# A decoder trunk on one Trainium2 core: each attention item's values product is issued four steps of the projection later, together with the next item's scores, and its output is taken two steps behind it

## The reference

```python
z = rms_norm(x, g_mix) @ w_in + b_in
q, k, v, u, vg = jnp.split(z, SPLITS, axis=-1)
scores = jnp.einsum('bnqhgd,bnshd->bnhgqs', qb, kb) * ATTN_SCALE      # 128-blocks, this one and the one before
probs = sink_softmax(scores, mask, sinks)
out = jnp.einsum('bnhgqs,bnshd->bnqhgd', probs, vb)
vg = layer_norm(gelu(vg), ...); gm_out = gelu(u) * chunk_spatial_mix(vg, gm_w_s, gm_b_s)
x = x + jnp.concatenate([attn_out, gm_out], axis=-1) @ w_out + b_out
```

## Time and profile before

| | |
|---|---|
| median of 3 runs | 986.0 us (lowest 985.79, highest 986.68) |
| profiled execution: its time / its span | 986.51 us / 984.8 us |
| TensorE busy | 963.6 us (98%) |
| VectorE, ScalarE, GpSimd busy | 672.4, 458.7, 260.5 us |
| the part that the change touches | about 416 to 515 us of the span |

### The profile page before, as it was taken

How to read it: one execution, slowest core, us unless ns; L and a number is a source line. 1 busy time by engine, 2 the same in 40 slices (tenths; PEclk the granted TensorE clock), 3 DMA queues, 4 the chain that set the end, 5 groups by cost and what they waited for, 6 DMA issues and landing times.

```text
span 984.8 us, 19296 instructions
## 1 busy us (share of the span) xinstructions
PE 963.6 (98%) x7949; PEld 947.1 (96%) x7949; DVE 672.4 (68%) x1063; ACT 458.7 (47%) x750; POOL 260.5 (26%) x150
## 2 busy tenths in 40 slices
PE   6999999999999999999999999999999999999997
PEld 4999999999999999999899999999999999999997
DVE  5899658856768654457775399857766758855576
ACT  6645425533435443566444455424543443545243
POOL 2302202211111226332318411301221211114521
PEclk9999999999999999999999999999999999999999
DMA  7962433252243336321114693253324325235202
GB/s 216 163 127 70 124 105 99 76 145 72 75 128 99 97 85 184 102 65 44 44 55 129 128 172 97 61 145 97 96 80 116 97 60 144 65 98 161 87 22 88
DMA packets 191603, 101.38 MB, mean 103 GB/s; under 512 B 12955, under 2 KB 189429, under 8 KB 191501
## 3 DMA queue, kind: packets, MB, share of 16 engines
q1 hardware_dynamic: 175904, 90.23, 32.2%
q0 software_dynamic: 11440, 5.77, 4.7%
q10 hardware_dynamic: 4172, 4.15, 1.4%
HBM read 97.59 MB, written 3.59 MB: 103 GB/s over the span
## 4 chain that ended last, share of the span: by engine, by line
PE 91%; DVE 5%; ACT 1%; DMA 1%; issue 1%; SPq 0%; DVEq 0%; ACTq 0%
PE ps L1723 49%; PE ps L1803 36%; PE ps L2141 2%; PE ps L1759 1%; DMA x_rows<-in_x_prompt_dram 1%; PE ps L2015 1%; PE ps L2044 1%; DVE w_lo L1327 0%; PE ps L1754 0%; DVE w_lo L1419 0%; PE ps L1748 0%; DVE xb_lo L1216 0%; DVE tt L1437 0%; DVE mix_lo L1550 0%; PE ps L2165 0%
## 5 line engine op out<-in xcount | busy, mean ns | idle before, releaser
L1803 PE MATMUL ps<-xo_hi,w_hi 128*128 128x260 f32 x1008 | 284.2, 282 | 0.7 <-DVE ab L1350 0.7
L1803 PE MATMUL ps<-xo_lo,w_hi 128*128 128x260 f32 x1008 | 284.7, 282 | 0.0
L1803 PE MATMUL ps<-xo_hi,w_lo 128*128 128x260 f32 x1008 | 284.4, 282 | 0.0
L1723 PE MATMUL ps<-h_hi,w_hi 128*128 128x260 f32 x960 | 195.8, 285 | 0.7 <-issue 0.6
L1723 PE MATMUL ps<-h_hi,w_lo 128*128 128x260 f32 x960 | 193.4, 283 | 0.0
L1723 PE MATMUL ps<-h_lo,w_hi 128*128 128x260 f32 x960 | 193.4, 283 | 0.0
L1803 PEld LDWEIGHTS ps<-xo_hi,w_hi 128*128 128x128 f32 x1008 | 189.6, 188 | 0.9 <-issue 0.9
L1803 PEld LDWEIGHTS ps<-xo_hi,w_lo 128*128 128x128 f32 x1008 | 189.8, 188 | 0.0
L1803 PEld LDWEIGHTS ps<-xo_lo,w_hi 128*128 128x128 f32 x1008 | 189.7, 188 | 0.0
L1723 PEld LDWEIGHTS ps<-h_hi,w_hi 128*128 128x128 f32 x960 | 148.1, 189 | 1.7 <-issue 1.2
L1723 PEld LDWEIGHTS ps<-h_lo,w_hi 128*128 128x128 f32 x960 | 148.8, 189 | 0.0
(11 more groups left out here) (276 smaller groups left out, 1476.5 us busy)
## 6 DMA issues: line engine op xcount, KB each, us to landing
w_raw<-in_w_ffn_dram SPq DMA_DIRECT2D x88, 256.0 KB, 3.0
w_a<-in_w_ffn_dram SPq DMA_DIRECT2D x36, 512.0 KB, 4.8
w_raw<-in_w_ffn_dram SPq DMA_DIRECT2D x48, 384.0 KB, 3.2
w_raw<-in_w_ffn_dram SPq DMA_DIRECT2D x16, 512.0 KB, 7.0
w_lo<-in_w_ffn_dram POOLq DMA_DIRECT2D x11, 512.0 KB, 8.4
w_raw<-in_w_in_dram SPq DMA_DIRECT2D x10, 512.0 KB, 4.0
w_raw<-in_w_ple_gate_dram SPq DMA_DIRECT2D x8, 512.0 KB, 3.6
x_rows<-in_x_prompt_dram SPq DMA_DIRECT2D x4, 512.0 KB, 5.7
```

Source lines behind the costliest of these rows:

```text
L1723: ins = pe.matmul(ps[:, bank + step * h, 0:HALF], w[:, c, w0:w0 + P], m_[:, sk, h * HALF:(h + 1) * HALF], start=(first and n == 0), stop=( ...
L1803: ins = pe.matmul(ps[:, b, 0:Q], w[:, c, k * P:(k + 1) * P], m_[:, op, k, :], start=(first and k == 0 and n == 0), stop=(k == 3 and n == 2 ...
```

## The change

The two last steps of each item are put elsewhere in the list: `values` from (u+1, 7) to (u+2, 3), `o_take` from (u+2, 2) to (u+2, 5). They are put in a loop of their own behind the first, and `put` inserts in front, so `values` of item i stands ahead of `scores` of item i+2 and `p_turn` of item i+1, and `o_take` ahead of `p_turn` r = 1 of item i+1. Behind line 320 every line number of the changed kernel is one higher.

```diff
         put(u + 1, 5, ("p_turn", i, 1))
-        put(u + 1, 7, ("values", i))
-        put(u + 2, 2, ("o_take", i))
+    for i, u in enumerate(ITEM_UNIT):
+        put(u + 2, 3, ("values", i))
+        put(u + 2, 5, ("o_take", i))
```

## The result

The changed kernel took 987.86 us (median of 22 runs, 986.2 to 989.05), the kernel before 986.07 on the same chip (22 runs, 985.09 to 988.01). The ratio is 1.0016, with a 95% interval of 1.0010 to 1.0023: 1.6 us slower (1.0 to 2.3). The forecast was 989.8, 3.8 slower, with a range of 987.0 to 992.3. So the sign was right and the time lies in the range, but the cost is less than half of what the sum gave, and it is inside the 0.2% for which I gave only 0.13.

What follows compares the result with a forecast made beforehand. TensorE was taken to bound up to 470 us, then mostly VectorE's mixer chain. Hand-over delays net of joins ended at +2.1, the half clock added 1.7: +3.8 on the median 986.0 gives 989.8 us, range 987.0 to 992.3.

Steps and rivals of the forecast that it cites:

- Joins: TensorE, items 0 to 5: values joined to scores in one insertion save 0.2 us each, -1.2 in all.
- The hand-over in units 7 and 9: o_take's copy behind L711 delays VectorE's remainder, soft and gelu_end; TensorE waits 1.5 us for g_t, twice.
- `ws_sum`, g3, `s_new`: Units 8 to 12: ws_sum waits 0.7 us, g3's turning comes 1.9 later, s_new 2.9 later, TensorE waits 1.8 for it.
- The last stretch: VectorE's part up to the release at 514.87: takes over the 2.9 us lag, less corrections, ending +2.1.
- The clock: TensorE at half clock behind its last wait, for mix_lo, where the chain is on TensorE: +1.7 us (0 to 1.9).
- The wait for `mix_lo`: TensorE, mixer's last stretch: grows from 1.0 to about 3 us, and half clock follows it.
- Rival (b): Hold-up as counted, but no half clock behind the last wait, or hidden as before: 988.1 us; chance 0.27.
- The sign that I had named: If the forecast waits are there and the time is under 988 us, the clock term is wrong.

Runs made afterwards that it cites:

- e6: Kernel of e2 with values at k-step 2 instead of 3, in an insertion of their own; 983.58 us, ratio 0.9971 to the kernel before.
- e2: Changed kernel with o_take split: ScalarE's copy stays at k-step 5, VectorE's remainder at k-step 7 behind the softmax; 982.13 us, again 982.05.
- e3: Changed kernel with values left in their old place (u+1, 7), only o_take moved to (u+2, 5); 988.37 us.
- e5: Kernel of e1 with the weights' split (w_hi, w_lo) at k-step 6 instead of 4 in all units; 992.92 us.
- e1: Changed kernel with o_take one k-step earlier, (u+2, 4) instead of (u+2, 5), so ScalarE's copy precedes the weights' copy; 987.71 us.
- e9: Kernel before, with only VectorE's remainder of the output moved to k-step 7 behind the softmax; values and ScalarE's copy left; 987.45 us.
- e7: Kernel before, with only the weights' split moved to k-step 6 instead of 4 in units 9 and 11; 988.35 us.
- e8: Kernel of e2 with the weights' split at k-step 6 instead of 4 in all units; 989.18 us.
- e4: Changed kernel with items 1, 3 and 5 left as before, only items 0, 2, 4, 6 and 7 changed; 986.39 us, ratio 0.9999.
- e10: Changed kernel once more, unaltered, one profiled execution to see where TensorE's clock falls; 986.92 us.

## Why the prediction was right or wrong

**Joins: right.** Item 1's values and item 3's scores, with the turning behind them, took 2.46 us of TensorE as one insertion (431.90 to 434.84, less two pairs of the projection at 0.24). Before, they took 1.22 (428.71 to 430.41) and 1.44 (432.79 to 434.71) apart, each less two pairs. That is 0.2 per join, as forecast. The time of e6 is in keeping with six of them.

**The hand-over in units 7 and 9: right in mechanism, in place and nearly in size.** Forecast two waits of 1.5 for `g_t`, measured two of 1.3. The profile counts the idle time from the end of the last pair of the projection; from start to start TensorE lost 1.44 us in unit 7 (the pair at 438.39, its 0.24, and 440.07), against 1.55. The difference is the link from L711 to what stands behind it: I took 1.09 us from the earlier trace rows, and it was 0.95 (435.60 to 436.55). I had misread that row: by TensorE's row the turning before it ended at 436.53 (435.93 + 0.60), so the copy that starts at 436.57 had most likely waited for TensorE, and not for L711 alone. e2 takes the link out and both waits go. e3 puts the values back under it and 1.0 of each goes. VectorE's L1493 was idle for 2.52 and 3.38 us, where 2 to 3 was forecast. The root of the argument stands. In unit 9 the long step of the earlier trace rows, now L1471, took 0.16, as expected, since `soft` came behind w_lo.

**`ws_sum`, g3, `s_new`: right, each a little too large.** The wait for the maxima was 0.5 (forecast 0.7), g3's turning came 1.69 later (1.9), `s_new` and with it `s_probs` 2.35 later (2.9). The wait for `s_new` was 1.4 (1.8).

**The last stretch: +2.1 was forecast, +1.37 measured.** The end of the mixer moved from 514.87 to 516.75, less 0.51. 0.55 of the gap was there before the stretch began, since `s_new` was 2.35 later and not 2.9. I had let that lag run through with two corrections. The trace shows more that happened in between. VectorE, before and after:

```profile
488.67 0.20 DVE L1596 TENSOR_TENSOR s_o<-ps,s_pv 128x64 f32<-128x64 f32 x1
...
492.64 1.70 DVE L1546 TENSOR_TENSOR sp<-sp,gu 128x520 f32<-128x520 f32 x1
494.26 1.21 DVE L1419 TENSOR_TENSOR w_lo<-w_raw,w_hi 128x1024 fp32r<-128x1024 f32 x1
```

```profile
490.54 0.40 DVE L1493 TENSOR_TENSOR mix_lo<-ps,mix_hi 128x256 fp32r<-128x256 f32 x1
490.87 1.45 DVE L1446 SCALAR_TENSOR_TENSOR gu<-tt 128x520 f32<-128x520 f32 x1
492.24 0.21 DVE L1597 TENSOR_TENSOR s_o<-ps,s_pv 128x64 f32<-128x64 f32 x1
...
496.11 0.70 DVE L1547 TENSOR_TENSOR sp<-sp,gu 128x520 f32<-128x520 f32 x1
496.73 1.22 DVE L1420 TENSOR_TENSOR w_lo<-w_raw,w_hi 128x1024 fp32r<-128x1024 f32 x1
...
503.76 0.42 DVE L1493 TENSOR_TENSOR mix_lo<-ps,mix_hi 128x256 fp32r<-128x256 f32 x1 [0.27 <-ACT mix_hi L972]
...
507.26 0.74 DVE L1536 SCALAR_TENSOR_TENSOR diag<-ps,cols,bs_all 128x512 f32<-128x512 f32 x1
```

Item 6's remainder (0.33 until the next starts) stood ahead of `s_o` before too, only earlier in the list, and costs nothing, as forecast. `gelu_end` met GpSimd's gv_rows (1.45 instead of 0.68), which I had not counted, and `s_o` is 3.06 later. But the gm product L1546, which met gv_rows before (1.70), does not meet it any more (0.70): at the w_lo behind it the lag is 1.96. I had seen that, and put 0.3 on it where it was 1.0. Item 7's `o_take` gives back 0.5, as forecast: at the last `spatial` the lag is 507.26 - 505.39 - 0.51 = 1.36. The step that failed was to carry a lag through VectorE without asking at each of its long rows whether GpSimd is still beside it. Here one meeting more and one less (+0.8 and -0.7 against the forecast) nearly cancel, which is luck.

**The clock: the term of 1.7 was wrong, and it is most of the error.** The half clock came, but elsewhere. Three stretches of after, around and behind the wait for `s_new` which ended at 482.97:

```profile
483.00:484.80 1.80, 1.80 (x14) 1.73 (x15) 1.56 (x6) 1.80 (x6) 0.00 (x0) 0.99 0.75 223
484.80:488.20 3.40, 3.40 (x22) 2.84 (x21) 3.02 (x16) 0.51 (x2) 0.00 (x0) 0.50 0.00 0
488.20:495.00 6.80, 6.60 (x57) 6.40 (x56) 4.47 (x11) 3.14 (x7) 5.97 (x4) 1.00 0.00 0
```

It lasted 3.4 us, as long as in the earlier trace rows, and cost TensorE 1.7 again. But it fell ahead of the wait for `s_o`, on which VectorE came last anyhow, and only ate that wait: 2.0 in the earlier trace rows, 0.2 now.

The wait for `mix_lo`, forecast at about 3, stayed at 0.9, so the case that I had priced did not arise. Three links failed. First, I had not asked whether the grown wait for `s_new` (forecast at 1.8 by my own sum) would bring a fall, though it comes first. Second, the 3 us do not follow from my own numbers. I still had TensorE waiting at `s_o`, so what it gained ahead of that can't count behind it. Behind it TensorE is spared 1.7 of half clock and VectorE's chain gets shorter by 2.9 - 2.1 = 0.8, which makes 1.0 + 1.7 - 0.8 = 1.9. Measured, the chain got shorter by 3.06 - 1.37 = 1.69, and 1.0 + 1.7 - 1.69 is about the 0.9 that was found. Third, I had inferred from one fall behind one wait that 3 us before `mix_lo` bring one. e5 had just that wait, 3.12 us, and no fall in the one execution that was profiled.

The two terms make up the whole gap within the mixer: 1.7 here and 0.7 up to the end of the last stretch, 3.8 forecast and 1.37 in the trace, and the ratio of the medians, 1.0 to 2.3 us, holds the latter. Rival (b) had the right shape, granted down earlier and hidden as before; its 988.1 lies 0.2 from the measured median, and I gave it 0.27. The sign that I had named, waits there and a time under 988, came out as it says, if only just: the clock term is wrong. The time lies in the stated range because the range had been drawn down to 987.0 for this rival, not because the forecast's own sum held.

**The rest.** From the end of the mixer to the end of the span the profiled execution of the changed kernel makes up 1.2 us on the one of before (VectorE's rows are 1.88 later at 516 us and 0.65 later at 911 us). 0.85 of that comes at 632 us, where the one of before waited for `ab` (0.75) and the changed one did not. Of the other executions profiled only the first of e2 shows this wait too (0.8). The second one of e2, the same kernel, does not. So it comes and goes between executions of one kernel, and I don't count it for the change. The other third was not followed up.

**What stays open** is what brings the clock down. Behind waits of 1.3 and 1.5 for `g_t` it never fell, nor behind 1.6 for `mix_lo` in e2. It fell behind 1.4 for `s_new` in the changed kernel and 1.66 in e1, behind 2.34 and 1.83 in e9. And it did not behind 3.12 in e5, though in the same execution it had fallen at 487 us (0.50 over 487 to 490), where the last waits were 0.44 and 0.50. The length of the wait before it alone does not order these cases, and most of them are one execution each.

## What to carry to other kernels

When an instruction that waits is moved, follow the queue behind it on its own engine before counting what the move saves on another: here a remainder of 0.34 us ahead of a softmax cost two waits of 1.3, and the same instruction behind the softmax made the change a gain of 3.5 to 4 us. A step's release has two sides, who stands behind it (the softmax) and who waits for its result (the next values, e9), and both need room. The remainder behind the softmax lost time as long as the values stood at the same k-step, and the move of the values lost time as long as the remainder stood ahead of the softmax. And an arrival that is earlier by less than the rest of an instruction that shuts it out is worth nothing (e1), while one that moves the neighbour may cost far more than the collision did (e5, e7, e8).

## What the runs showed of the hardware

A GpSimd instruction of 2.4 us stretches some VectorE steps that meet it, however small they are: 128x4 steps from 0.17 to 1.32 (e1), 2.33 (e4) and 2.25 (e9), one from 0.15 to 2.27 (e7), and four scalings of 128x128 from 1.01 to 3.12 (e5), each up to about the end of w_lo. The loss is the rest of GpSimd's instruction. All of these have every operand in SBUF. Steps that read PSUM were not stretched: in unit 7 of the changed kernel L1493 (0.43) and the four maxima L1463 (0.48 each) ran wholly beside w_lo (436.73 to 439.14) at their usual length. Neither was the first layer-norm step `BATCH_NORM_STATS2`, which reads SBUF (five of them from 445.05 in 1.05 us before, w_lo from 445.48). When VectorE is in the middle of its own row, GpSimd can be the one that is stretched (2.38 to 2.71 in e2, which starts inside `gelu_end`).

TensorE's clock stayed at its full level of 2.4 GHz through and behind an idle stretch of 3.12 us (e5, one execution), and was at half for 3.4 us behind one of 1.41 (after, and at the same place in e10). I had taken the longer wait for the more dangerous one.
